# A mixture-of-experts layer: routing table of 256 columns built tile by tile, no second pass for overflow rows, six weight pieces fetched before the experts start

## The reference, cut to what matters

```
p_group = softmax(xf @ w_rg + b_rg);  p_top, g_idx = top_k(p_group, 1)      # 4 groups
le_sel  = logits of the 8 experts of that group;  top_l, e_loc = top_k(le_sel, 2)
gate    = softmax(top_l) * p_top                                            # 2 experts for each of 1024 tokens
# the 2048 (token, expert) pairs are sorted by expert, padded per expert to blocks of 128 rows
hid = silu(xb @ w_eg[e]) * (xb @ w_eu[e]);  ys = hid @ w_ed[e]              # one block of one expert
out = rmsnorm(x2 + sum of the two gated rows of each token)
```

## Time and profile before

| | |
|---|---|
| median of 3 runs | 1251.81 us (1249.84 to 1252.39) |
| profiled execution, its own time | 1248.3 us |
| its span in the trace | 1246.0 us |
| PE busy | 1114.2 us, 89% of the span |
| DVE busy | 726.3 us, 58% |
| ACT busy | 564.2 us, 45% |
| POOL busy | 325.3 us, 26% |

### The profile page before, as it was taken

How to read it: one execution, slowest core, us unless ns; L and a number is a source line. 1 busy time by engine, 2 the same in 40 slices (tenths; PEclk the granted TensorE clock), 3 DMA queues, 4 the chain that set the end, 5 groups by cost and what they waited for, 6 DMA issues and landing times.

```text
span 1246.0 us, 18300 instructions
## 1 busy us (share of the span) xinstructions
PE 1114.2 (89%) x6865; PEld 963.8 (77%) x6865; DVE 726.3 (58%) x920; ACT 564.2 (45%) x759; POOL 325.3 (26%) x272
## 2 busy tenths in 40 slices
PE   3998999999999899999998999767999999999940
PEld 3876888888877788888887777657999999999930
DVE  5875666666055611111115444477888888888838
ACT  5335556555144200000003222345787888888823
POOL 3103322113222223333320001022444444444210
PEclk7998999999999999999998999878999999999975
DMA  7010000021204111111113341286899999999737
GB/s 244 2 28 11 7 7 11 3 69 35 51 1 111 34 34 51 51 50 37 50 51 90 119 169 68 76 308 254 310 366 358 344 347 358 359 382 364 277 143 287
DMA packets 94172, 184.29 MB, mean 148 GB/s; under 512 B 30752, under 2 KB 68128, under 8 KB 80288
## 3 DMA queue, kind: packets, MB, share of 16 engines
q1 hardware_dynamic: 83744, 166.65, 38.5%
q0 software_dynamic: 10368, 16.80, 3.7%
HBM read 177.12 MB, written 27.26 MB: 164 GB/s over the span
## 4 chain that ended last, share of the span: by engine, by line
PE 73%; DVE 13%; ACT 5%; issue 3%; DMA 2%; SPq 2%; POOL 1%; DVEq 0%; ACTq 0%; POOLq 0%
PE ps L372 22%; PE ps L374 21%; PE ps L373 21%; PE ps L905 2%; PE ps L668 2%; PE ps L828 1%; DVE pt_lo L1385 1%; DVE negm L1340 1%; DVE we_lo L1634 1%; SPq L351 1%; DVE x L1494 1%; ACT prob L1035 1%; DVE q_tmp L1331 1%; DVE acc L1686 1%; DVE res L1696 1%
## 5 line engine op out<-in xcount | busy, mean ns | idle before, releaser
L1634 DVE TENSOR_TENSOR we_lo<-raw_e,we_hi 128x2048 fp32r<-128x2048 f32 x108 | 246.9, 2288 | 54.6 <-ACT we_hi L1162 54.6
L1162 ACT ACTIVATE we_hi<-raw_e 128x2048 fp32r<-128x2048 f32 x108 | 205.8, 1908 | 0.0
L372 PE MATMUL ps<-ht_hi,w_hi 128*128 128x512 f32 x448 | 176.1, 393 | 0.4 <-DVE ht_lo L1258 0.4
L374 PE MATMUL ps<-ht_hi,w_lo 128*128 128x512 f32 x448 | 174.5, 389 | 0.0
L373 PE MATMUL ps<-ht_lo,w_hi 128*128 128x512 f32 x448 | 174.4, 389 | 0.0
L372 PE MATMUL ps<-we_hi,xst_hi 128*128 128x256 f32 x576 | 169.4, 294 | 2.4 <-DVE xst_lo L1638 2.4
L373 PE MATMUL ps<-we_lo,xst_hi 128*128 128x256 f32 x576 | 163.3, 283 | 0.0
L374 PE MATMUL ps<-we_hi,xst_lo 128*128 128x256 f32 x576 | 163.2, 283 | 0.0
L366 POOL CAST w_hi<-raw 128x1024 fp32r<-128x1024 f32 x36 | 40.6, 1127 | 302.8 <-PE ps L374 270.6
L372 PEld LDWEIGHTS ps<-we_hi,xst_hi 128*128 128x128 f32 x576 | 111.1, 193 | 2.8 <-DVE xst_lo L1638 2.8
L373 PEld LDWEIGHTS ps<-we_lo,xst_hi 128*128 128x128 f32 x576 | 111.0, 193 | 0.0
(11 more groups left out here) (286 smaller groups left out, 2505.5 us busy)
## 6 DMA issues: line engine op xcount, KB each, us to landing
raw_e<-in_w_exp_gate_dram SPq DMA_DIRECT2D x36, 1024.0 KB, 9.1
raw_e<-in_w_exp_up_dram SPq DMA_DIRECT2D x36, 1024.0 KB
raw_e<-in_w_exp_down_dram SPq DMA_DIRECT2D x36, 1024.0 KB, 9.1
raw<-in_w_in_dram SPq DMA_DIRECT2D x27, 512.0 KB, 3.9
yin<-y_dram SPq DMA_DIRECT2D x16, 512.0 KB, 6.6
xin<-in_x_dram SPq DMA_DIRECT2D x8, 512.0 KB, 7.2
raw<-in_w_out_dram SPq DMA_DIRECT2D x8, 512.0 KB, 4.0
xre<-in_x_dram SPq DMA_DIRECT2D x8, 512.0 KB, 4.3
```

Source lines behind the costliest of these rows:

```text
L372: pe.matmul(dst, st[0], mv[0], start=first, stop=False)
L374: return pe.matmul(dst, st[1], mv[0], start=False, stop=last)
L1162: act.activation(we_hi[c % 4][:, :], raw_e[c % 6][:, :], ACT.Copy).then_inc(sem("w_hi_ready"), 1)
L1634: dve.tensor_tensor(we_lo[c % 4][:, :], raw_e[c % 6][:, :], we_hi[c % 4][:, :].bitcast(F32), ALU.subtract).then_inc(sem("w_lo_ready"), 1)
```

## The change

1. **One table of 256 columns.** `LV = 8` levels of 32 experts: column `level * 32 + expert` holds the pairs with rank 128*level to 128*level + 127. `place` finds level and row of each pair, and `sel_b` becomes 128x512 for both choices (8 levels x 32 experts). There is one value in the table, the output row; the token is worked out of it (1024 less where it is 1024 or more). `sel_a`, `sel_b`, `oe` have one buffer each instead of two or eight.
2. **Order in stage W.** `place(t-1)` stands on DVE directly behind `rows_out(t)`, ahead of `normed(t)`; `table(t-2)` stands on PE after n = 9, behind `router(t-1)`, which now waits until `place(t-2)` has read its counts. For the last tile `table(6)` stands behind the loop.
3. **No second pass.** `overflow_rows`, `overflow_table` and the last read are gone. `overflow_blocks` reads the other 224 columns and makes, for each overflow block, the expert and the column of the table; two small PE transposes turn them into rows (PE waits for `blocks_summed` between `rows_in(0)` and the first `columns`), and `block_numbers` writes `blk_e` and `blk_c`.
4. **Columns by register.** In the loop POOL loads the column's number from `blk_c` into a register, twice per block (gather, scatter).
5. **Weights.** Six pieces are loaded in stage W (three at tile 3, three at tile 6). The wait for the first gather ahead of the sixth piece is gone, and so later loads wait only for their slot. The rows of blocks 2 and 3 lie in other places, so POOL clears them between its first gathers.

```diff
-                if t >= 2:
-                    dve.wait_ge(sem("sel_used"), t - 1)
-                link(dve.tensor_tensor(sel_b[t % 2][:, :, :, :], oe..., val..., ALU.mult))
+                link(dve.tensor_tensor(oev[:, :, :], oe[:, :, :], val[:, t, :].unsqueeze(2).to_broadcast([P, 2, NE]), ALU.mult))
...
             def place(t):
                 dve.wait_ge(sem("rank_done"), t + 1)
                 link(prod = oe * counts); link(rk = sum of prod)
-                dve.tensor_tensor(sel_a[t % 2][:, :, :], iota_row..., rk..., ALU.is_equal).then_inc(sem("sel_ready"), 1)
+                link(above = rk >= 128, 256, ...); link(ob = sum of above)
+                link(rr = rk - 128 * ob); link(level = (0..7 == ob))
+                if t:
+                    dve.wait_ge(sem("sel_used"), t)
+                link(sel_b = level x oev)
+                dve.tensor_tensor(sel_a[:, :, :], iota_row..., rr..., ALU.is_equal).then_inc(sem("sel_ready"), 1)
...
                 rows_out(t, 0, 2)
+                if t:
+                    place(t - 1)
                 normed(t)
                 if t + 2 < NT:
                     mt_low(t + 2)
-                if t:
-                    place(t - 1)
                 route(t)
...
-                        if n == 5 and t >= 2:
+                        if n == 9 and t >= 2:
                             table(t - 2)
...
-            dve.tensor_scalar(xidx[:, 0:NE], ps[:, 7, 0:NE], NONE, None, ALU.add).then_inc(sem("tab_read"), 1)
+            link(dve.tensor_scalar(tabf[:, primary], ps[:, 7, primary], NONE, None, ALU.add))
+            link(dve.tensor_scalar(past[:, primary], tabf[:, primary], float(T), -float(T), ALU.is_ge, ALU.mult))
+            dve.tensor_tensor(xidx[:, primary], tabf[:, primary], past[:, primary], ALU.add).then_inc(sem("tab_read"), 1)
...
                 rows_in(0, 0)
+                pe.wait_ge(sem("blocks_summed"), 1)
+                for i in range(2):
+                    mm = pe.transpose(ps[0:1, 6, 128 + i * P:128 + (i + 1) * P], bsum[:, i:i + 1], ident[:, :])
+                mm.then_inc(sem("blocks_turned"), 1)
                 columns(0, 0, 0)
...
-                    if isinstance(it, int) and j < 2:
-                        overflow_rows(j)
-                    if isinstance(it, int) and j == 2:
-                        overflow_table()
...
+                    if t == NT - 2:
+                        sp.wait_ge(sem("mt_lo_ready"), NT)
+                        load(1, 0, 1); load(2, 0, 0); load(0, 0, 2)
...
-                sp.wait_ge(sem("rt_done"), NT)
-                load(2, 0, 0)
-                load(0, 0, 2)
-                sp.wait_ge(sem("xs_full0"), 16)
-                sp.wait_ge(sem("ediff_ready"), 1)
-                sp.wait_ge(sem("totals_done"), 1)
-                load(1, 0, 1)
...
+                    return bass.ds(pool.value_load(blk_c[0:1, bass.ds(it * 4 + j, 1)], min_val=0, max_val=EMPTY), 1)
```

More of the change, by code:

```diff
@@ L230, in build @@
         gne = at("gne", 35.6875, [P, G], F32)
-        lmask = at("lmask", 35.75, [P, NE], F32)
-        prod = at("prod", 204, [P, 2, NE], F32)
-        sel_b = [at(f"sel_b{i}", 204.25 + i / 2, [P, 2, 2, NE], F32R) for i in range(2)]
-        sel_a = [at(f"sel_a{i}", 205.25 + i, [P, 2, P], F32R) for i in range(2)]
-        r_at = [176.0]
+        above = at("above", 35.71875, [P, 2, 7], F32)
+        lmask = at("lmask", 35.78125, [P, NE], F32)
+        level = at("level", 35.90625, [P, 2, LV], F32)
+        prod = at("prod", 1.5, [P, 2, NE], F32)
+        oe = at("oe", 1.75, [P, 2, NE], F32)
+        oev = at("oev", 5.25, [P, 2, NE], F32)
+        sel_b = at("sel_b", 204, [P, 2, LV, NE], F32R)
+        sel_a = at("sel_a", 206, [P, 2, P], F32R)
+        r_at = [205.0625]
         def scratch(name, shape, dt=F32):
@@ L837, in ranks @@
                         pe.wait_ge(sem("cum_ready"), t)
-                    mm = pe.matmul(ps[:, 6, 128:128 + NE], before[:, :], oe_b[t % 2][:, :], start=True, stop=t == 0)
+                    dst = ps[:, 6 if t < NT - 2 else 0, 128:128 + NE]
+                    mm = pe.matmul(dst, before[:, :], oe_b[t % 2][:, :], start=True, stop=t == 0)
                     if t:
-                        mm = pe.matmul(ps[:, 6, 128:128 + NE], ones_b[:, :], cum_b[:, t, :], start=False, stop=True)
+                        mm = pe.matmul(dst, ones_b[:, :], cum_b[:, t, :], start=False, stop=True)
                     mm.then_inc(sem("rank_done"), 1)
@@ L889, in _ @@
                 pe.matmul(ps[:, 6, 64:64 + NE], ones_b[:, :], oe_b[LAST % 2][:, :], start=False, stop=True).then_inc(sem("totals_done"), 1)
-                def overflow_table(k):
-                    pe.wait_ge(sem("osel_ready"), k + 1)
-                    for t in range(NT):
-                        mm = pe.matmul(ps[:, 7, 64:96], osel_a[:, t, :], osel_b[:, t, :, :].rearrange("p a b -> p (a b)"),
-                                       start=t + k == 0, stop=t == NT - 1 and k == 1)
-                    mm.then_inc(sem("osel_used"), 1)
             if "E" in on:
@@ L1534, in place @@
                 def place(t):
                     dve.wait_ge(sem("rank_done"), t + 1)
-                    link(dve.tensor_tensor(prod[:, :, :], oe[:, :, t, :], ps[:, 6, 128:128 + NE].unsqueeze(1).to_broadcast([P, 2, NE]), ALU.mult))
-                    link(dve.tensor_reduce(rk[:, :, t], prod[:, :, :], AX, ALU.add))
-                    dve.tensor_tensor(sel_a[t % 2][:, :, :], iota_row[:, :].unsqueeze(1).to_broadcast([P, 2, P]),
-                                      rk[:, :, t].unsqueeze(2).to_broadcast([P, 2, P]), ALU.is_equal).then_inc(sem("sel_ready"), 1)
+                    counts = ps[:, 6 if t < NT - 2 else 0, 128:128 + NE]
@@ new lines, in place @@
+                    link(dve.tensor_tensor(prod[:, :, :], oe[:, :, :], counts.unsqueeze(1).to_broadcast([P, 2, NE]), ALU.mult))
+                    link(dve.tensor_reduce(rk[:, :], prod[:, :, :], AX, ALU.add))
+                    link(dve.tensor_tensor(above[:, :, :], rk[:, :].unsqueeze(2).to_broadcast([P, 2, 7]),
+                                           steps_of_p[:, 0:7].unsqueeze(1).to_broadcast([P, 2, 7]), ALU.is_ge))
+                    link(dve.tensor_reduce(ob[:, :], above[:, :, :], AX, ALU.add))
@@ L1670, in _ @@
                 low(0, 0, 1)
+                block_numbers()
                 rows_low(0, 1)
@@ L1782, in expert, with clear @@
                     if left(4):
+                        c = column(it, j + 4)
                         pool.wait_ge(sem("xs_tr"), it * 4 + (j + 1))
-                        gather(it, j + 4)
-                    if isinstance(it, int) and j == 3:
-                        pool.wait_ge(sem("tab_read"), 4)
+                        gather(it, j + 4, c)
                     scatter(it, j)
+                def clear(j):
+                    pool.memset(xs[j][:, :], 0.0).then_inc(sem("xs_clear"), 1)
+                    pool.wait_ge(sem("xs_clear"), j + 1)
                 pool.wait_ge(sem("mt_lo_ready"), NT)
-                for j in range(4):
-                    pool.memset(xs[j][:, :], 0.0).then_inc(sem("xs_clear"), 1)
-                pool.wait_ge(sem("xs_clear"), 4)
+                clear(0)
+                clear(1)
                 for i in range(2):
@@ L1797, in _ @@
                 for j in range(4):
+                    if j == 2:
+                        pool.wait_ge(sem("out_done"), NT + 1)
+                        pool.wait_ge(sem("rt_done"), NT)
+                    if j >= 2:
+                        clear(j)
                     rows_at(0, j, xidx[:, j:j + 1])
-                pool.wait_ge(sem("tab_read"), 2)
                 experts(pool, expert)
```

154 lines of the change are left out of this document (79 added, 75 removed).

## The result

The changed kernel takes 1237.63 us (median of 4 runs, 1234.7 to 1238.95) against 1250.82 us for the kernel before on the same chip (median of 4 runs, 1247.45 to 1252.39): a ratio of 0.9895, interval 0.9866 to 0.9923. I had said 1235.0 us, 1230 to 1242. The profiled execution of the changed kernel took 1234.7 us with a span of 1232.8 us, against 1248.3 and 1246.0.

A forecast was written before the change was run, and what follows sets the result against it. PE bounds the loop, so gains come only from its waits and slow clock: -7.0 - 0.8 + 2.3 + 1.0 + 0 - 12.3 = -16.8 us, profile about 1231.5; 3.5 more for the median gives 1235.0 us, range 1230 to 1242.

The forecast's parts named there:

- What bounds it: PE fills 9.88 of 10 us in the loop; gains only at waits for `sel_a` (6.3 us) and `hidt_lo` (12.8 us).
- Middle tiles, -7.0: Stage W, five middle tiles: `place` early ends PE's waits for `sel_a`, -7.0 us, bounds -6.3 and -7.1.
- Last tile, -0.8: Last tile of stage W: tables no longer ahead of router and projection's last half, -0.8 us, bounds 0 and -1.0.
- Last counts to gather, +2.3: Uncovered path before the first gather: longer `place(7)`, wider table matmuls, three instructions for one, +2.3 us, bounds 1.9 and 2.8.
- First gather, +1.0: Issue of first gather to PE's start: slowed by a weight load in flight, +1.0 us, bounds 0 to 3.6.
- my own signs: Listed signs of a wrong forecast, among them a first gather that lands more than 7 us after its issue.
- `blocks_summed`, 0: PE's new wait before the first `columns`: costs 0, with 0.8 us of cover, since `xst_lo` starts later anyway.
- Early pieces, 0: Six weight pieces loaded early gain nothing in the first block, since ACT's order holds their conversion back.
- Overflow passes, -12.3: Blocks 1 to 3: without the second pass no `hidt_lo` wait and no clock drop, -12.3 us.
- the rival of half the gain: Blocks gain 6 instead of 12.3 us because a slip brings back wait and slow clock: 1241 us, chance 0.13.
- Register loads, 0: POOL's two register loads per block fit in its 4.12 us of idle time: 0.
- the rival on the slower side: POOL becomes the loop's bound if a register load takes more than 2.1 us: 1266 us at 2.6 each, chance 0.05.

The follow-up runs named there:

- experiment 1: The kernel before with only the new order in stage W, tables as they were: 1242.82 us, ratio 0.9935.
- experiment 2: The kernel before without `overflow_rows` and `overflow_table` and nothing in their place, so overflow rows are left out: 1241.44 and 1236.42 us, no ratio.
- experiment 9: The changed kernel with `place(t-1)` back behind `mt_low` on DVE, the table still behind the router: 1255.09 us, ratio 1.0038.
- experiment 3: The changed kernel with the second three weight pieces loaded as late as before: 1232.95 us, ratio 0.9858.
- experiment 4: The changed kernel with SP's wait for the first gather put back behind the six early pieces: 1231.76 us, ratio 0.9836.
- experiment 12: The changed kernel with SP's first-gather wait, `gates()` moved early, and POOL's clearing of two row buffers behind DVE's table reading: 1227.59 us, ratio 0.9815.
- experiment 7: The changed kernel with SP's first-gather wait, `gates()` moved early, and early-piece conversions ahead of work that waits for rows: 1227.73 us, ratio 0.9824.
- experiment 10: The changed kernel with three more register loads ahead of each of POOL's two per block: 1233.3 us, ratio 0.9893.
- experiment 11: The changed kernel with six more register loads ahead of each of POOL's two per block: 1234.37 us, ratio 0.9898.
- the second: Second profile of the changed kernel, run again unchanged: a profiled execution of 1227.34 us; those runs had median 1235.08 us, ratio 0.9896.

## Why the prediction was right, point by point

**What bounds it**: confirmed. The steady loop didn't move (its scatters are 9.9 to 10.0 us apart before and after), and both of the waits that I named gave the gain; experiments 1 and 2 show each alone.

**Middle tiles, -7.0**: 1.5 us each, -7.5 in all. The mechanism is right and the term 0.5 short. That the new order needs `place` early, and that the router's new wait turns dear without it, is shown by experiment 9. My estimate of `place`, 2.5 us for eight instructions, is 800.00 to 802.47 in the changed profile. **Last tile, -0.8**: -0.93.

**Last counts to gather, +2.3**: +1.74 against the old profile. Experiments 1 and 2 have 9.0 us where that had 9.41, so against those the change costs 2.15 us; the old profile's 0.4 us belong to its execution.

**First gather, +1.0**: +1.69, inside the bounds of 0 to 3.6. My +1.0 was a choice between these bounds, and 0.7 short; by my own signs, a gather of more than 7 us spoke against the forecast. Experiments 3 and 4 show the cause that I gave, loads in flight. By the Trainium skill's rule of a packet from each queue in turn ("DMA: Bandwidth & Descriptors", Queues, rings and completion order) I had estimated a loss of up to 3.2 us; the runs give 1.8, between my choice and that limit.

**`blocks_summed`, 0**: nothing to be seen in the changed profile, but the cover was thinner than I said: with rows 1.8 us earlier the wait appears (1.41 us). One instruction of the chain, `past`, took 1.63 us where I had about 0.4; the conclusion survived, and experiments 4 and 12 show why, as PE waits for `xst_lo` behind it in any case.

**Early pieces, 0**: confirmed by experiments 3 and 4. Experiment 7 shows an order of ACT and DVE that uses them.

**Overflow passes, -12.3**: -12.8, and -12.9 in experiment 2. Full clock came back at once, as I had assumed; the rival of half the gain is out.

**Register loads, 0**: confirmed with a wide margin by experiments 10 and 11, which removes the rival on the slower side. The Trainium skill's floor of about 0.6 us for a `tensor_load` ("DMA: Bandwidth & Descriptors", Latency and other measured facts) would make 8.4 us of fourteen, by my estimate, twice POOL's idle time. The trace doesn't agree with such a cost in POOL's own time: the blocks kept their length, and seven loads leave no gap ahead of `xcol`. Whether a load is shorter or runs beside POOL's other work the runs don't say.

**The sum**: 1231.5 us for a profile, 1234.7 in the first and 1227.34 in the second. The step that was not in my sum at all is the clock behind waits that the change leaves alone: +1.6 in the first tile, +1.05 and +0.85 in block 0 in the first profile, and next to nothing of these in the second. The terms that I named came to -17.8 and not -16.8, and these three places took 3.5 back, so that the median came out only 2.6 us above the forecast is in part luck. So is the step from profile to median: I took +3.5 us from the old runs, and it was +2.9. One sum in the prediction is wrong: from 1251.8 the bounds as they are written there give 1233.3 to 1239.6, not 1232 to 1238.5. It changes nothing, since the stated range was taken wider.

**What stays open**: why the clock falls behind a wait, or comes back, sooner in one execution than in the next. At the start of stage W the same wait of 3.24 us for `mt_lo` is followed by half clock in some profiles and not in others. In block 0 the waits ahead of it are alike in both profiles of the changed kernel (9.07 and 9.03 us for the rows, 1.94 and 1.94, 3.80 and 3.80).

## What to carry to other kernels

Cost a wait of PE together with the clock behind it, and read that from the trace: here a wait of 1.24 us cost 1.4, one of 1.50 us cost 3.3, and cutting 3.8 to 2.5 us gave twice what was cut. Half clock costs only where PE is what the next step waits for: in the first tile it was free in seven profiles and cost 1.6 us in seven. Before a load is sent earlier, look at which engine's order decides when it is used, and at the small urgent transfer that it may share the queues with. Where the parts of a change are to be compared at the level of 2 us, cut the traces at common events: whole times of one kernel here spread over 12 us.

## What the runs showed of the hardware that I had not expected

A DVE `TENSOR_SCALAR` from SBUF to SBUF (128x224, float32) took 1.63 us beside a POOL MEMSET and 0.28 us ahead of it; instructions of the same width that read PSUM took 0.38 to 0.39 in both cases. The Trainium skill ("SBUF — State Buffer", SBUF: two separate sides) says that DVE in a two-port mode and POOL take one pair of ports by an exclusive lock for a whole instruction. The trace agrees that one waits for the other: `past` ends at 810.55, 0.14 us after the MEMSET. By the recorded starts, though, `past` was first by 0.5 us and would have had to win; starts on POOL are rough, and no run here settles that, nor whether `past` ran in such a mode.
